# Forget-gate weights: upper and lower parts in one stationary tile, two matmuls a tile in place of three

## The reference

```
z = rms_norm(x, g_norm) @ w_in            # fa: 16 columns of z, one for each head
log_f = log_sigmoid(fa + b_f)             # 256 tokens x 16 heads
c = cumsum(log_f, axis=tokens)
s = q k^T * scale + c[t] - c[s]           # the gate's part in forgetting attention
```

## Time and profile before

| what | value |
|---|---|
| median of 3 runs | 774.57 us (774.33 to 774.76) |
| span of the profiled execution (first to last instruction) | 773.1 us; its whole time is not given apart |
| TensorE busy | 764.9 us (99%) |
| VectorE, ScalarE, GpSimd busy | 516.4, 409.7, 230.6 us |
| forget gate's 24 matmuls | 53.06 to 55.90 us |
| granted clock of TensorE | 0.999 of full speed |

### The profile page before, as it was taken

How to read it: one execution, slowest core, us unless ns; L and a number is a source line. 1 busy time by engine, 2 the same in 40 slices (tenths; PEclk the granted TensorE clock), 3 DMA queues, 4 the chain that set the end, 5 groups by cost and what they waited for, 6 DMA issues and landing times.

```text
span 773.1 us, 12621 instructions
## 1 busy us (share of the span) xinstructions
PE 764.9 (99%) x5057; PEld 661.9 (86%) x5057; DVE 516.4 (67%) x775; ACT 409.7 (53%) x663; POOL 230.6 (30%) x182
## 2 busy tenths in 40 slices
PE   9999999999999999999999999999999999999997
PEld 7889987899877889987778888998888888888885
DVE  5748765665667648866457965788788676777553
ACT  6645357634487444343335545736857555556451
POOL 3031796750751000055019910126001111011010
PEclk9999999999999999999999999999999999999999
DMA  9899995397621654554545556440464556655741
GB/s 234 200 250 227 256 220 131 85 206 176 162 83 55 235 173 144 187 191 151 150 132 164 187 194 191 137 138 29 140 215 138 184 174 214 190 177 178 238 171 54
DMA packets 78140, 130.70 MB, mean 169 GB/s; under 512 B 4478, under 2 KB 28274, under 8 KB 77954
## 3 DMA queue, kind: packets, MB, share of 16 engines
q1 hardware_dynamic: 76640, 124.96, 55.8%
q0 software_dynamic: 1200, 4.83, 2.0%
q10 hardware_dynamic: 242, 0.11, 0.0%
HBM read 128.82 MB, written 1.06 MB: 168 GB/s over the span
## 4 chain that ended last, share of the span: by engine, by line
PE 98%; DVE 1%; ACT 1%; issue 0%; DVEq 0%; ACTq 0%
PE ps L1666 15%; PE ps L1670 15%; PE ps L1674 15%; PE ps L1724 10%; PE ps L1707 6%; PE ps L1711 6%; PE ps L1703 6%; PE ps L1732 5%; PE ps L1802 2%; PE ps L1818 2%; PE ps L1833 2%; PE ps L2187 1%; PE ps L2064 1%; PE ps L1595 1%; PE ps L2016 1%; PE ps L2072 1%
## 5 line engine op out<-in xcount | busy, mean ns | idle before, releaser
L1011 DVE TENSOR_TENSOR w_lo<-stage,w_hi 128x1024 fp32r<-128x1024 f32 x224 | 294.0, 1336 | 157.7 <-ACT w_hi L664 157.2
L664 ACT ACTIVATE w_hi<-stage 128x1024 fp32r<-128x1024 f32 x230 | 239.0, 1060 | 234.0 <-PE ps L1674 104.0
L1666 PE MATMUL ps<-w_hi,act_t 128*128 128x512 f32 (+1 forms) x368 | 100.4, 395 | 0.2 <-ACT act_t L691 0.2
L1674 PE MATMUL ps<-w_lo,act_t 128*128 128x512 f32 (+1 forms) x368 | 96.5, 385 | 0.0
L1724 PE MATMUL ps<-act_t,w_hi 128*128 128x512 f32 x352 | 84.1, 391 | 0.0
L1674 PEld LDWEIGHTS ps<-w_lo,act_t 128*128 128x128 f32 x368 | 68.1, 188 | 14.0
L1666 PEld LDWEIGHTS ps<-w_hi,act_t 128*128 128x128 f32 x368 | 66.5, 188 | 15.3 <-issue 2.5
L1670 PE MATMUL ps<-w_hi,act_t 128*128 128x512 f32 (+1 forms) x304 | 79.5, 384 | 0.0
L1724 PEld LDWEIGHTS ps<-act_t,w_hi 128*128 128x128 f32 x352 | 64.7, 188 | 12.7
L1670 PEld LDWEIGHTS ps<-w_hi,act_t 128*128 128x128 f32 x304 | 56.1, 188 | 11.6
L1703 PE MATMUL ps<-act_t,w_hi 128*128 128x256 f32 x416 | 58.9, 284 | 0.0
(11 more groups left out here) (384 smaller groups left out, 1167.3 us busy)
## 6 DMA issues: line engine op xcount, KB each, us to landing
stage<-in_even_w_in SPq DMA_DIRECT2D x62, 512.0 KB, 5.5
stage<-in_odd_w_in SPq DMA_DIRECT2D x48, 512.0 KB, 4.0
stage<-in_w_gate_up SPq DMA_DIRECT2D x44, 512.0 KB, 4.7
stage<-in_w_down SPq DMA_DIRECT2D x22, 512.0 KB, 4.3
stage<-in_even_w_out SPq DMA_DIRECT2D x16, 512.0 KB, 3.8
stage<-in_odd_w_out SPq DMA_DIRECT2D x16, 512.0 KB, 3.9
stage<-in_w_in SPq DMA_DIRECT2D x10, 512.0 KB, 3.8
stage<-in_w_out SPq DMA_DIRECT2D x8, 512.0 KB, 5.1
```

The source lines that it names most:

```text
L664: nc.scalar.activation(w_hi[:, u % RING, :], stage[:, u % RING, :], ACT.Copy).then_inc(hi_ready, 1)
L1011: nc.vector.tensor_tensor(w_lo[:, u % RING, :], stage[:, u % RING, :], w_hi[:, u % RING, :].bitcast(F32), ALU.subtract).then_inc(lo_ready, 1)
L1666: mm(out[:, b, :], a_hi(k)[:, tok[b]], hi[:, i, :], start=(k == 0), stop=False)
L1674: ins = mm(out[:, b, :], a_hi(k)[:, tok[b]], lo[:, i, :], start=False, stop=(k == k_tiles - 1))
```

## The change

`wf_hi` and `wf_lo` are replaced by one tile `wf_both` with 64 columns for each tile of the contraction: the upper part in columns 0 to 15, the lower part in columns 32 to 47, zeros between. A stationary operand of 128 columns from column 64 k on then holds both parts of tile k (and of tile k + 1, whose results are not used). One matmul with `x_hi(k)` and one with `x_lo(k)` make the sums of both parts: rows 0 to 15 of bank 4 hold the upper weights' product, rows 32 to 47 the lower weights'. (The lower weights with the lower activations, which were left out before, are in it now.) ScalarE copies rows 32 to 47 into a part of the gate's buffer, and VectorE adds the two before the norm factor. The fill at the start covers all of `wf_both`, 576 columns, where it covered 112.

```diff
-        W_F = KD * FOX_H + P - FOX_H
-        wf, wf_hi, wf_lo = sb("wf", [P, W_F]), sb("wf_hi", [P, W_F], F32R), sb("wf_lo", [P, W_F], F32R)
+        W_F = P // 2
+        wf, wf_both = sb("wf", [P, KD * FOX_H]), sb("wf_both", [P, (KD + 1) * W_F], F32R)
+        wf_part = lambda at: wf_both[:, 0:KD * W_F].rearrange("p (k c) -> p k c", c=W_F)[:, :, at:at + FOX_H]
+        wf_of = wf[:].rearrange("p (k h) -> p k h", k=KD)
...
-                        nc.scalar.activation(wf_hi[:], wf[:], ACT.Copy).then_inc(wf_hi_ready, 1)
-
+                        nc.scalar.activation(wf_part(0), wf_of, ACT.Copy).then_inc(wf_hi_ready, 1)
+
+            act.wait_ge(f_done, 1)
+            nc.scalar.activation(gate_f[:, 2], ps[32:32 + FOX_H, 4 * BANK:4 * BANK + S], ACT.Copy).then_inc(f_low, 1)
             split_hi(chunks[("qa", 1)][0] + 1)
...
-            nc.vector.memset(wf[:, KD * FOX_H:W_F], 0.0)
+            nc.vector.memset(wf_both[:].bitcast(F32), 0.0)
             nc.vector.memset(neg_half[:], -0.5).then_inc(fills, 1)
...
-                    TT(wf_lo[:], wf[:], wf_hi[:].bitcast(F32), ALU.subtract).then_inc(wf_lo_ready, 1)
+                    TT(wf_part(32), wf_of, wf_part(0).bitcast(F32), ALU.subtract).then_inc(wf_lo_ready, 1)
...
             dve.wait_ge(f_done, 1)
+            dve.wait_ge(f_low, 1)
             f_in, f_neg = gate_f[:, 0], gate_f[:, 1]
-            then(TT(f_in, ps[0:FOX_H, 4 * BANK:4 * BANK + S], rstd_row[0:FOX_H, :], ALU.mult))
+            then(TT(f_in, ps[0:FOX_H, 4 * BANK:4 * BANK + S], gate_f[:, 2], ALU.add))
+            then(TT(f_in, f_in, rstd_row[0:FOX_H, :], ALU.mult))
...
-                w = slice(k * FOX_H, k * FOX_H + P)
-                passes = ((wf_hi[:, w], x_hi(k)), (wf_lo[:, w], x_hi(k)), (wf_hi[:, w], x_lo(k)))
-                for n, (left, right) in enumerate(passes):
-                    ins = mm(bank(4, S), left, right, start=(k == 0 and n == 0), stop=(k == KD - 1 and n == 2))
+                w = wf_both[:, k * W_F:k * W_F + P]
+                mm(bank(4, S), w, x_hi(k), start=(k == 0), stop=False)
+                ins = mm(bank(4, S), w, x_lo(k), start=False, stop=(k == KD - 1))
```

More of the change, by code:

```diff
@@ L274, in build @@
         c_wide_ready, c_turned, c_ready = sem("c_wide_ready"), sem("c_turned"), sem("c_ready")
-        wf_hi_ready, wf_lo_ready, f_done, f_abs, f_exp, f_ln = (sem(n) for n in ("wf_hi_ready", "wf_lo_ready", "f_done", "f_abs", "f_exp", "f_ln"))
+        wf_hi_ready, wf_lo_ready, f_done, f_low, f_abs, f_exp, f_ln = (sem(n) for n in ("wf_hi_ready", "wf_lo_ready", "f_done", "f_low", "f_abs", "f_exp", "f_ln"))
         cum_ready, v_block_ready = sem("cum_ready"), sem("v_block_ready")
@@ L474, in _ @@
             pool.wait_ge(unit_used, FORGET_AT)
-            pool.dma_start(wf[:, 0:KD * FOX_H].rearrange("p (k h) -> p k h", k=KD), w_even[:, :, even_at["fa"]:even_at["fa"] + FOX_H]).then_inc(wf_in, 16)
+            pool.dma_start(wf_of, w_even[:, :, even_at["fa"]:even_at["fa"] + FOX_H]).then_inc(wf_in, 16)
             pool.wait_ge(unit_used, PARAMS_AT)
```

## The result

The changed kernel takes 775.62 us in the median of 20 executions (774.57 to 779.72), the kernel before 774.65 (774.24 to 775.35). The ratio is 1.0015 [1.0008, 1.0022]: 1.0 us slower, 0.6 to 1.7. Forecast were 774.05 us and a range of 773.3 to 774.9; the time lies outside it. The highest of the 20, 779.72 us, had a mean granted clock of 0.994 where the others had 0.998 to 1.000. The profiled execution took 775.73 us, so 1.8 us lie around its span, 0.3 more than the 1.47 I had added.

What follows compares the result with a forecast made beforehand. TensorE, busy 764.9 of 773.1 us, was taken to bound the kernel. Span 773.1 - 0.95 (gate's block) + 0.43 (start) = 772.58, plus 1.47 around it, gave 774.05 us, 0.52 less; range 773.3 to 774.9.

Steps and rivals of the forecast that it cites:

- does it come late: Whole kernel: TensorE is nearly always busy, so work of other engines was costed only if it made TensorE wait.
- up to 0.2%, 1.55 us: Whole kernel's time: a difference within some 0.2%, 1.55 us, can't be told from no change; "same" got 0.91.
- TensorE's block: Gate's block on TensorE: 24 matmuls become 16 at 0.118 us each, 0.95 us less (0.92 to 1.02).
- rival D: Gate's block: second matmul on a stationary tile costs other than the first; under 0.1 us; 0.72 together with the forecast.
- The fill: VectorE's third memset at the start grows from 112 to 576 elements, delaying TensorE's first matmul by 0.50 us.
- the forecast 0.43 on the path: Start: of the fill's 0.50 us, 0.43 reaches TensorE's path through the vectors' transpose and first weight unit; bounds 0 to 0.50.
- rival C: Start: TensorE's faster level comes later and reaches past the first weight unit, + 2.8 us, 776.85; chance 0.04.
- Rival A: Start: the longer fill costs nothing, as data land later or early matmuls run faster; 773.6 us; chance 0.13.
- ScalarE and VectorE at the gate: Gate: ScalarE's added copy takes 0.42 us, VectorE's addition 0.45 to the next start; both covered, so zero cost.
- rival B: Behind the gate: the fourth qa unit's lower half comes late and takes the gain; 774.1 to 775.0 us; chance 0.09.
- the tightest cover: Fourth qa unit's lower half: ready at 65.1, asked for at 66.1; covered by 1.0 us, or 0.6 if VectorE starts late.
- a cover of 1.0 us: Unit after the fourth qa unit: VectorE's lower half ends at 68.0 and TensorE asks for it at 69.0.

Runs made afterwards that it cites:

- e9: Kernel before with 448 unused bytes a partition ahead of the tiles behind the gate's weights; 775.86 us, ratio 1.0016.
- e1: Changed kernel with 64 unused bytes a partition behind wf_both, so later tiles start at their old addresses; 774.09 us, ratio 0.9991.
- e4: Kernel before with a second zero fill of 464 elements a partition ahead of the fill that releases TensorE; 775.13 us, ratio 1.0004.
- e6: Changed kernel with old addresses restored by 64 unused bytes and wf_both's zero fill moved behind the fill that releases TensorE; 773.98 us, ratio 1.0000.
- e8: Kernel before with 64 unused bytes a partition ahead of its very first tile, so all tiles move together; 774.80 us, ratio 1.0001.
- e11: Kernel before with act_t and what stands behind it moved by 64 bytes, the work region by 512; 778.10 us, ratio 1.0045.

## Why the prediction was wrong

**The step that failed** is the one by which everything outside TensorE's own block was read "only as 'does it come late'", with the busy 506.57 of 507.00 us as the reason. That finds matmuls that wait, not matmuls that each take longer. The new sizes of the gate's tiles were in the diff (`W_F`), and what they do to the tiles behind them was not among the edits that I costed: a term of +1.25 us (worked out from the steps; 1.27 measured alone in e9) was missing from a sum of -0.52. With it the sum is 775.3, and with the 0.20 us of the matmuls behind `y_lo` 775.5; e1, which takes both out, came to -0.74 us, and -0.52 lies inside its interval. That a change of up to 0.2%, 1.55 us, can't be told from none was too wide as well: 20 executions of each kernel told 1.0 us from nothing.

**TensorE's block: right.** 16 matmuls in 1.88 us, 0.118 each, as forecast; 0.96 us gone where I had 0.95. The second matmul on one stationary tile costs what the first does; rival D is out.

**The fill: right at VectorE, too dear behind.** In the chain the 576 elements take 0.54 us, the 112 took 0.12: 0.42 more. TensorE's first matmul starts at 1.70 and not 1.22, 0.48 later. The fill's own row grew by 0.39 us, from 152 ns to 538, and it began 0.10 later (1.09, 0.99 before). The Trainium skill, page "VectorE: DVE Perf Modes", section "Zero memsets can be issued as uint32 (trn2)", with its cycle an element gave an estimate of 0.48 for the 464 at the clock that the prediction names; the trace agrees in the delay, not in the row's duration.

Of the forecast 0.43 on the path only 0.17 arrived at the first weight unit. The timeline after (columns as in the earlier trace rows):

```profile
5.42 1.29 PE L1601 MATMUL ps<-ident,x 128*128 128x128 f32 x8
...
6.37 0.84 ACT L693 ACTIVATE act_t<-ps,col 128x256 fp32r<-128x256 f32 x2 [3.01 <-PE ps L1601]
...
9.03 0.76 PEld L1694 LDWEIGHTS ps<-w_hi,act_t 128*128 128x128 f32 x4 [0.48 <-ACT w_hi L658]
```

ScalarE's `act_t` came at 6.37 where it came at 6.20, the second group of the first unit at 9.03 and not 8.86. The early matmuls went over to the quicker pace at 5.9 us and not 6.8, and that gave back the rest. I had let the pace change only for the worse (rival C). This is TensorE's clock. The trace's record of the granted clock has its first entry, full speed, at 6.80 us before and at 5.92 after, at the matmul where the step falls from 213 to some 110 ns, and so it is in all 14 profiles. Ahead of that entry nothing is recorded, and the 1.00 of the earlier trace rows over the start, which the prediction quotes, says nothing of the slow passes; that these ran at the lower level, 1.2 GHz, is worked out from steps of nearly two to one. In the profiles of this case the entry stands between 4.2 and 6.8 us; what sets the moment no run here shows, so one profile can't price the start; by the times (e4) it lies between -0.3 and +1.0 us. Rival A, a start that costs nothing, is neither shown nor excluded.

**ScalarE and VectorE at the gate: right in the durations, one cover too generous.** The rows of ScalarE and then of VectorE that answer to the earlier trace rows:

```profile
57.26 1.24 ACT L763 ACTIVATE gate_b<-ps,rstd 128x512 f32<-128x512 f32 x2
58.52 0.38 ACT L771 ACTIVATE lag<-ps 16x256 f32<-16x256 f32 x1
58.81 2.10 ACT L666 ACTIVATE w_hi<-stage 128x1024 fp32r<-128x1024 f32 x2
...
64.04 0.42 ACT L774 ACTIVATE lag<-lag 16x256 f32<-16x256 f32 x1 [1.83 <-DVE lag L1168]
```

```profile
62.33 0.41 DVE L1165 TENSOR_TENSOR lag<-ps,lag 16x256 f32<-16x256 f32 x1
62.77 0.41 DVE L1166 TENSOR_TENSOR lag<-lag,rstd_row 16x256 f32<-16x256 f32 x1
...
64.25 1.23 DVE L1015 TENSOR_TENSOR w_lo<-stage,w_hi 128x1024 fp32r<-128x1024 f32 x1
...
67.28 3.46 DVE L1015 TENSOR_TENSOR w_lo<-stage,w_hi 128x1024 fp32r<-128x1024 f32 x3
```

The copy took 0.38 us (0.42 taken) without a wait, the addition 0.44 to the next start (0.45). VectorE reached it at 62.33 where it had been at 61.93, and its lower halves of the next chunk began at 67.28, 0.84 late. TensorE, which the shorter block brings there 0.85 us earlier, stood 0.11 us for the first of them: the row x8 of 1.07 us above. So rival B came true in small and one unit later than the tightest cover I had named. To this unit the prediction gave a cover of 1.0 us, by 68.0 against 69.0. VectorE was later than that: the addition's 0.45 was in the sum, but not the 0.40 by which VectorE came late to the gate's steps (the 0.43 of the start was reckoned with for the fourth unit alone), and the first of the three halves ended at 68.46. TensorE was earlier: 0.85 us ahead and not 0.52, and it loads a tile some 0.12 us before the matmul that uses it (69.22 and 69.33 for this one before, where the sum went by 69.5).

**Rival C.** Its mechanism, a faster level that comes at another moment, is what the start showed, but to the good side in this profile. On the bad side three executions would fit: the 779.72 us above and e6's 777.72 and 777.55, 3.6 to 4.1 us over their medians, each at a mean granted clock of 0.994, and none of the 20 of the kernel before. None of the three was profiled, so whether it is rival C, and whether the change makes it more likely, isn't shown.

**Still open.** Why a distance of 64 or 128 bytes between the two tiles lengthens the step, why that reaches into the matmuls behind, and why the short form prefers another distance, no run here shows.

## What to carry to other kernels

When an edit changes the size of a tile, it moves every tile behind it: look at where those stand against their partners before and after, and keep the distance the same with a few unused bytes, or measure the others. When a kernel bound by TensorE gains less than the instructions taken out, compare the duration and the step of the matmuls that were *not* touched, group by group, before looking for a wait. A start-up whose length varies by itself between profiles is priced by many timed runs, not by one trace.

## What the runs showed of the hardware

Matmuls of fp32r tiles with 512 moving columns and the six tiles stationary step at 227.4 ns at the distance that the kernel before has between stationary and moving tile, and at 256 and 512 bytes more; at 229.6 with 64 bytes less, at 233.7 with 64 more and at 233.0 with 128 more. Moving both tiles together by 64 bytes changes nothing (e8). The slowing reaches into matmuls right behind whose own tiles did not move (226.7 to 229.9 ns behind `y_lo`). The 256-column form goes the other way in e11: with the stationary tile 64 bytes lower nearly all single steps of line 1732 are 113 to 118 ns where nearly all were 119 to 120. 64 bytes in one place of the allocation, with no other change, were worth up to 3.5 us of 775.

TensorE's step for one form halved, from 213 to some 110 ns, at the first entry of full speed in the trace's clock record, 4.2 to 6.8 us into the span.
